# Two layers of sixteen experts: where the sums back to the tokens stand, the last pair as whole fp32 numbers, and the order of the layer norm behind them

## The reference, cut to what matters

```python
def _expert_choice_ffn(u, w_router, w_g, w_u, w_d):
    cap = CAPACITY_FACTOR * n // N_EXPERTS          # 64 tokens for each of 16 experts
    aff = softmax(einsum('bnd,de->ben', u, w_router), axis=1)
    gate, idx = lax.top_k(aff, cap)
    xe = u[bidx, idx]
    hg, hu = einsum(xe, w_g), einsum(xe, w_u)
    ye = einsum(silu(hg) * hu, w_d) * gate[..., None]
    return jnp.zeros_like(u).at[bidx, idx].add(ye)
...
h = _layer_norm(ALPHA * h + m[5] * experts(h), ln_ffn_g, ln_ffn_b)     # end of layers 0 and 1
...
hn = rmsnorm(h, attn_norm[0]); h = h + hybrid_ab(hn, ...)              # first step of the second network
```

## Time and profile before

| what | value |
|---|---|
| time, median of 3 runs | 2934.12 us (2933.55 to 2934.4) |
| span of the profiled execution | 2932.9 us |
| mean granted PE clock | 0.975 |
| PE busy | 2717.6 us, 93% |
| DVE / ACT / POOL busy | 1156.8 / 813.5 / 119.7 us |
| chain that ended last | PE 75%, DMA 12%, DVE 8%, ACT 3% |

### The profile page before, as it was taken

How to read it: one execution, slowest core, us unless ns; L and a number is a source line. 1 busy time by engine, 2 the same in 40 slices (tenths; PEclk the granted TensorE clock), 3 DMA queues, 4 the chain that set the end, 5 groups by cost and what they waited for, 6 DMA issues and landing times.

```text
span 2932.9 us, 32767 instructions
## 1 busy us (share of the span) xinstructions
PE 2717.6 (93%) x13760; PEld 1779.9 (61%) x13760; DVE 1156.8 (39%) x1700; ACT 813.5 (28%) x1249; POOL 119.7 (4%) x120
## 2 busy tenths in 40 slices
PE   6898899998899989998879999999999999999998
PEld 4555444433378544343337777878778766787886
DVE  4465512211264442111135654323244577532333
ACT  3253211100132121100024324212232467532222
POOL 1211100000000200000010010000010000000000
PEclk8999999999999989999999999999999899999999
DMA  8980799999922189999982203231341200132220
GB/s 305 325 282 16 284 415 428 427 422 421 419 99 108 44 342 424 423 419 428 428 329 92 86 29 115 72 124 57 107 130 41 69 1 1 65 115 86 95 85 36
DMA packets 125586, 601.03 MB, mean 205 GB/s; under 512 B 7408, under 2 KB 12848, under 8 KB 100608
## 3 DMA queue, kind: packets, MB, share of 16 engines
q1 hardware_dynamic: 120128, 584.27, 50.3%
q0 software_dynamic: 5312, 14.68, 1.6%
HBM read 596.83 MB, written 2.10 MB: 204 GB/s over the span
## 4 chain that ended last, share of the span: by engine, by line
PE 75%; DMA 12%; DVE 8%; ACT 3%; issue 1%; POOL 0%; DVEq 0%; ACTq 0%; POOLq 0%
PE psum L302 72%; DMA weight_ring<-in_w_exp_down 4%; DMA scratch<-in_w_exp_down 4%; PE psum L317 4%; ACT scratch L290 3%; DVE scratch L252 3%; DMA scratch<-in_w_exp_up 2%; DMA weight_ring<-in_w_exp_up 2%; DMA weight_ring<-in_w_mod 1%; DVE scratch L265 1%; DVE scratch L3773 1%; DVE h L252 1%; DVE scratch L1448 0%; DVE scratch L1947 0%; DVE scratch L1945 0%
## 5 line engine op out<-in xcount | busy, mean ns | idle before, releaser
L302 PE MATMUL psum<-scratch,scratch 128*128 128x512 f32 (+12 forms) x9404 | 1869.6, 397 | 64.7 <-DVE scratch L252 18.4
L302 PEld LDWEIGHTS psum<-scratch,scratch 128*128 128x128 f32 (+5 forms) x9404 | 1365.2, 178 | 539.3 <-issue 203.6
L302 PE MATMUL psum<-weight_ring,scratch 128*64 128x512 f32 (+2 forms) x2752 | 649.7, 612 | 71.8 <-DMA weight_ring<-in_w_exp_down 29.8
L290 ACT ACTIVATE scratch<-psum 128x512 f32<-128x512 f32 (+5 forms) x384 | 221.6, 577 | 1037.7 <-PE psum L317 554.8
L302 PEld LDWEIGHTS psum<-weight_ring,scratch 128*64 128x64 f32 (+2 forms) x2752 | 210.0, 141 | 457.7 <-issue 372.5
L252 DVE TENSOR_TENSOR scratch<-weight_ring,scratch 128x2048 fp32r<-128x2048 f32 (+2 forms) x110 | 241.9, 2199 | 480.2 <-ACT scratch L290 478.6
L290 ACT ACTIVATE scratch<-weight_ring 128x2048 fp32r<-128x2048 f32 (+2 forms) x122 | 218.7, 1793 | 570.3 <-PE psum L302 547.2
L252 DVE TENSOR_TENSOR scratch<-scratch,psum 128x512 f32<-128x512 f32 x92 | 63.3, 688 | 511.8 <-PE psum L302 510.4
L252 DVE TENSOR_TENSOR scratch<-scratch,scratch 128x512 fp32r<-128x512 f32 (+13 forms) x359 | 198.3, 552 | 63.1 <-ACT scratch L290 43.2
L317 PE MATMUL psum<-consts,scratch 128*128 128x128 f32 x1116 | 168.5, 291 | 37.1 <-DVE scratch L252 20.2
L252 DVE TENSOR_TENSOR scratch<-psum,scratch 64x512 f32<-64x512 f32 (+7 forms) x109 | 77.6, 712 | 306.8 <-PE psum L302 302.3
(11 more groups left out here) (107 smaller groups left out, 721.7 us busy)
## 6 DMA issues: line engine op xcount, KB each, us to landing
weight_ring<-in_w_exp_down SPq DMA_DIRECT2D x46, 2048.0 KB, 13.8
weight_ring<-in_w_exp_up SPq DMA_DIRECT2D x43, 2048.0 KB, 15.7
weight_ring<-in_w_exp_gate SPq DMA_DIRECT2D x42, 2048.0 KB, 15.7
weight_ring<-in_ffn_w SPq DMA_DIRECT2D x28, 2048.0 KB, 7.7
weight_ring<-in_w_mod SPq DMA_DIRECT2D x24, 2048.0 KB, 9.6
scratch<-in_w_exp_gate SPq DMA_DIRECT2D x22, 2048.0 KB, 15.8
scratch<-in_w_exp_up SPq DMA_DIRECT2D x21, 2048.0 KB, 15.8
scratch<-in_w_exp_down SPq DMA_DIRECT2D x18, 2048.0 KB, 14.2
```

Of the source, the lines that this page charges most:

```text
L290: A.eng.activation(out, in_, fn, **kw).then_inc(*A.mark(*names))
L302: ins = T.eng.matmul(out, lhsT, rhs, start=start, stop=stop)
```

## The change: what it does

The way back has now two parts beside the experts, and its last pairs are handled apart. A sum (`plus_pe`) also multiplies pair 6 (experts 12 and 13, split as before) into its bank. Two of the sums stand before the down product of expert 14, two before that of expert 15, two behind it, and the last two among the jobs. Pair 7 (experts 14 and 15) is not split: DVE multiplies the down product by row and slot gate in one instruction, and each job ends in one whole fp32 product of `slotsT` and `y`. For that the slot gates of pair 7 must lie on both halves of the partitions, and `gates_pe` makes them by 16 products instead of 4. Sums 4 to 7 name their banks instead of taking the next ones in turn. In the norm of the second layer `gained` of the tile before moves between `stats` and `finish`; `mean` and `diagonals` of tile 0 move ahead of `finish` of tile 3. POOL adds the bias of tiles 0 and 1 only, DVE that of tiles 2 and 3, and POOL makes `units.lo` of the first unit instead of DVE. ACT makes `units.hi` of it behind the norm of tile 0.

```diff
@@ -836,8 +836,6 @@
 class SumNorm(PostNorm):
-    POOLED = NT - 1
-
     def normed(self, t):
@@ -858,15 +856,14 @@
             self.stats(V, t)
+            if after and t == NT - 1:
+                after.mean(V, 0, 1)
+                after.diagonals(V, 0, 1)
+            elif after and t:
+                self.gained(V, t - 1)
             self.finish(V, t)
-            if not after:
-                continue
-            if t == NT - 1:
-                after.mean(V, 0, 1)
-            if t:
-                self.gained(V, t - 1)
         if after:
-            after.diagonals(V, 0, 1)
+            self.gained(V, NT - 2)
             self.gained(V, NT - 1)
@@ -1612,7 +1609,7 @@
-    PARTS = ((0, 4), (4, 6), (6, 8))
+    PARTS = ((0, 4), (4, 6))
     AHEAD = 6
@@ -1691,6 +1688,8 @@
                 yield "turned", (e + 1) // 2
+            if e == E - 1:
+                yield from (("plus", j) for j in jobs[:2])
             if e:
@@ -1703,9 +1702,9 @@
                 yield from (("back", (1, *j)) for j in jobs[4 * (e - 13):4 * (e - 12)])
-        yield from (("plus", j) for j in jobs[:2])
+        yield from (("plus", j) for j in jobs[2:4])
         yield "down", E - 1
-        yield from (("plus", j) for j in jobs[2:self.AHEAD])
+        yield from (("plus", j) for j in jobs[4:self.AHEAD])
         yield from (("back", (2, *j)) for j in jobs)
@@ -1904,19 +1903,18 @@
             {"slots": self.slots_act, "up": self.up_act, "flip": self.flip_act, "rows": self.rows_act, "turned": self.turned_act}.get(what, self.nothing)(A, e)
-        self.down_act(A, E - 1)
         after = self.after
         for t in range(NT):
-            if after and t == NT - 1:
-
+            self.norm.norm_act(A, t)
+            if after and t == 0:
+                after.units.hi(A, 0)
+            if after and t == NT - 2:
                 A.wait_ge(*k.at("end", self.end_key, "pe"))
                 after.square(A, 0)
-            self.norm.norm_act(A, t)
+                after.root(A, 0, 1)
         if after:
-            after.root(A, 0, 1)
             after.square(A, 1)
             after.square(A, 2)
-            after.units.hi(A, 0)
             after.root(A, 1, 3)
@@ -1975,8 +1973,8 @@
                 after.diagonals(V, t0, t1)
-            after.units.lo(V, 0)
             after.chunks_dve(V)
+            V.wait_ge(*k.at("unit split", after.units.n0))
             after.units.lo(V, 1)
@@ -1993,6 +1991,7 @@
                 self.norm.norm_pool(G, t)
+            self.after.units.lo(G, 0)
         G.end(self.end_key)
@@ -2083,6 +2082,15 @@
         pair = 4 * g + pr
+        if pair == E // 2 - 1:
+            for e in range(2):
+                for half in range(2):
+                    for t in range(NT):
+                        end = t == NT - 1
+                        mm(T, bank[64 * half:64 * half + 64, 2 * e:2 * e + 2],
+                           self.onehot[g][:, t, pr * P + 64 * e:pr * P + 64 * e + 64].bitcast(F32), self.aff[:, t, 2 * pair:2 * pair + 2],
+                           t == 0, end, *([("full", key, "gates", *job)] if end and e and half else []))
+            return
         for t in range(NT):
@@ -2093,7 +2101,8 @@
         V.wait_ge(*k.at("full", key, "gates", *job))
-        copy(V, self.slot_gate[:, 2 * pair:2 * pair + 2], k.psum.of((key, "gates", *job))[:, 0:2], ("free", key, "gates", *job))
+        own = slice(0, 4, 3) if pair == E // 2 - 1 else slice(0, 2)
+        copy(V, self.slot_gate[:, 2 * pair:2 * pair + 2], k.psum.of((key, "gates", *job))[:, own], ("free", key, "gates", *job))
     def slots_pe(self, T, t):
@@ -2220,15 +2225,15 @@
             rows_, cols = slice(64 * half, 64 * half + 64), slice(half * HALF, (half + 1) * HALF)
-            tt(V, self.y[q, cols], k.psum.of((key, "down", e))[rows_, :], self.row[rows_, cols], ALU.mult, (key, "y", e, half),
-               *([("free", key, "down", e)] if half else []))
+            names = [(key, "y", e, half)] + ([("free", key, "down", e)] if half else [])
+            out, bank, row = self.y[q, cols], k.psum.of((key, "down", e))[rows_, :], self.row[rows_, cols]
+            if e >= E - 2:
+                stt(V, out, bank, self.slot_gate[rows_, e:e + 1], row, ALU.mult, ALU.mult, *names)
+            else:
+                tt(V, out, bank, row, ALU.mult, *names)
+        if e >= E - 2:
+            return
         hi, lo, y, gate = self.y_parts(e)
-        if e == E - 1:
-            for half in range(2):
-                s = slice(4 * half, 4 * half + 4)
-                V.wait_ge(*k.at(key, "y hi", e, half))
-                stt(V, lo[:, s], y[:, s], gate, hi[:, s].bitcast(F32), ALU.mult, ALU.subtract, (key, "y split", e, half))
-            return
         V.wait_ge(*k.at(key, "y hi", e))
@@ -2237,33 +2242,51 @@
         i, t, half = job
+        if i == len(self.PARTS):
+            name = (self.end_key, "out", t, half)
+            if 2 * t + half >= self.AHEAD:
+                self.plus_pe(T, (t, half))
+            T.wait_ge(*k.at(self.key, "y", E - 1, half))
+            mm(T, k.psum.of(name), self.slotsT[:, E // 2 - 1, t * P:(t + 1) * P].bitcast(F32), self.y[:, half * HALF:(half + 1) * HALF],
+               False, True, ("full", *name))
+            return
         p0, p1 = self.PARTS[i]
-        T.wait_ge(*k.at(self.key, "y split", 2 * p1 - 1, *([half] if p1 == E // 2 else [])))
+        T.wait_ge(*k.at(self.key, "y split", 2 * p1 - 1))
         T.wait_ge(*k.at("free", self.key, "slots", t, 0))
         T.wait_ge(*k.at("free", self.key, "slots", t, 1))
-        last = i == len(self.PARTS) - 1
-        name = (self.end_key, "out", t, half) if last else (self.end_key, "part", *job)
-        if last and 2 * t + half >= self.AHEAD:
-            self.plus_pe(T, (t, half))
-        bank = k.psum.of(name) if last else k.psum.take(T, name)
+        name = (self.end_key, "part", *job)
+        self.pairs_pe(T, k.psum.take(T, name), p0, p1, t, half, True, ("full", *name))
+
+    def pairs_pe(self, T, bank, p0, p1, t, half, first, *names):
+
         for pair in range(p0, p1):
...
             end = pair == p1 - 1
-            mm(T, bank, s, self.high[:, pair, 4 * half:4 * half + 4, :], pair == p0 and not last, False)
-            mm(T, bank, s, self.low_of(pair)[:, half * HALF:(half + 1) * HALF], False, end, *([("full", *name)] if end else []))
+            mm(T, bank, s, self.high[:, pair, 4 * half:4 * half + 4, :], pair == p0 and first, False)
+            mm(T, bank, s, self.low_of(pair)[:, half * HALF:(half + 1) * HALF], False, end and bool(names), *(names if end else ()))
     def plus_pe(self, T, job):
...
         T.wait_ge(*k.at(self.end_key, "back", 1, t, half))
-        bank = k.psum.take(T, (self.end_key, "out", t, half))
+        i = 2 * t + half
+        if i == 0:
+            self.first_bank = k.psum.turn[0, 8]
+        own = {4: 7, 5: 3, 6: 2, 7: 6}.get(i)
+        if own is None:
+            bank = k.psum.take(T, (self.end_key, "out", t, half))
+        else:
+            b = (self.first_bank + own) % 8
+            bank = k.psum.take(T, (self.end_key, "out", t, half), (b, b + 1))
         mm(T, bank, k.ident, k.h[:, t, half * HALF:(half + 1) * HALF], True, False)
+        T.wait_ge(*k.at(self.key, "y split", E - 3))
+        self.pairs_pe(T, bank, E // 2 - 2, E // 2 - 1, t, half, False)
```

10 lines of the change are left out of this document (3 added, 7 removed).

## The result

| | before | after |
|---|---|---|
| time, median of 8 runs each | 2933.84 us | 2943.73 us (2937.58 to 2945.09) |
| ratio | | 1.0027, 95% interval 1.0019 to 1.0036 |
| span of the profiled execution | 2932.9 us | 2943.3 us |
| PE / DVE / ACT / POOL busy | 2717.6 / 1156.8 / 813.5 / 119.7 us | 2727.2 / 1153.3 / 809.0 / 121.9 us |

The change makes the kernel slower by 0.27%. Laid on the 2934.12 us of the front, the ratio gives 2942.0 us (2939.7 to 2944.7). The forecast was 2939.0. So 2942.0 lies above the forecast's own 2937.5 to 2940.5 and on the very edge of the stated range of 2934.0 to 2942.0. By the forecast's own bound of 2940.0 slower came, to which it gave 0.26; the lower end of the interval, 2939.7, lies just under that bound.

The account below looks back on a forecast made before the run. PE was busy 93% of the span, so time was won or lost only where PE stands still. 0.6 + 4.4 = 5.0 us on 2932.9 gave 2937.9, 2939.1 with the 1.2 around it, stated as 2939.0; range 2934.0 to 2942.0.

Parts of the forecast that it names:

- The norm: Second layer's norm: DVE's shifts of tiles 1 and 2 and tile 0's diagonal wait for POOL; 4.4 us later.
- The first rival: Second layer's norm: small shifts go free, only the diagonal is held; +2.8 us, 2937.5 in all; chance 0.15.
- the second: Second layer's norm: DVE and POOL do not hold each other up; -0.1 us, 2934.1 to 2934.6; chance 0.17.
- Ahead of the last down product: End of the expert layers: costlier sums make the last down product end 0.86 us later in the first, 1.20 in the second.
- Behind it: Last down product to first statistics: two sums and a job instead of four sums and a job, 0.92 us less.
- The gates: Slot gates of pair 7 at expert 8: 3.0 us more PE work per layer, covered by waits for weights; taken as 0.
- The turning over: Behind the first layer: PE waits for a bank of tile 3 with twelve transposes behind it; 0.6 us later.
- PE cold: Second layer's products on the diagonals: longer pause leaves PE's clock low; up to 4.4 us more, likelier 2941.2; chance 0.18.
- The 1.2 us around the span: Whole kernel: difference between the span (2932.9) and the median of the runs (2934.12), taken to stay.
- The sum: Whole kernel: 0.6 us for the first layer's turning over plus 4.4 for the second layer's norm, 5.0 in all.

Follow-up runs that it names:

- e9: The changed kernel with shifts as an instruction with one SBUF tensor input and the first unit's low part on DVE, not POOL; norm 21.64 us, second stretch 58.96 us.
- e6: The changed kernel with only DMA issues on POOL in the second layer's closing stretch, DVE doing its work; norm 23.64 us, second stretch 59.64 us.
- e4: The kernel before with only the norm's part of the change; ratio to the kernel before 1.0023 (1.0014 to 1.0033).
- b2: The kernel before with DVE adding the bias of tile 2 and ACT making the unit's high part behind the norm of tile 1; ratio 1.0000.
- e5: The changed kernel with its last four sum banks in another order and the ring's turn moved on by one; first stretch 47.28 us, second 66.18 us.
- e1: The changed kernel with each shift made by an instruction with one SBUF tensor input instead of two; norm 24.47 us, second stretch 62.43 us.
- e1_finish_first: The changed kernel with each tile's reciprocal and shift ahead of `gained` of the tile before; norm 26.04 us, second stretch 61.80 us.

## Why the prediction was right and where it was off

- *The norm*: the mechanism named is the one that the runs show. The shifts are held until POOL ends, the diagonal ends with POOL's 128x2048 (4.50 us, as worked out), and e9, which takes away only the two overlaps, gives back 4.25 of 4.68. The size needs care, since the forecast's 4.4 has the 0.28 of the later statistics in it. From the first statistics on it stands for 4.1, and measured is 25.89 - 21.2 = 4.7, 0.6 more. Up to the statistics of tile 3 it was 3.70 for the forecast's 3.6. The stalls were smaller than priced (1.59 and 1.97 for 2.1 to 2.2 each), but DVE still waited 0.56 for ACT's root ahead of the first. The rest of the 0.6 came behind, most of it between the diagonal's end and PE's run (6.84 for 6.5).
- *The first rival* (small shifts go free) is refuted by the rows at 1529.11 and 1534.52, *the second* (DVE and POOL do not hold each other) by these and the one at 1540.20, and by e6.
- *Ahead of the last down product*, 0.86 and 1.20 us: mis-sized. By up piece to sums it was 0.5 (24.61 to 25.12) and 0.6 (24.88 to 25.49). The new sums stand 1.43 apart as priced (1498.32 to 1499.75), so more of them than I allowed lay in waits for weights. With the next term the statistics thus start 0.35 sooner in the first layer (forecast 0.06 sooner) and 0.25 sooner in the second (forecast 0.28 later).
- *Behind it*, -0.92: measured 4.67 to 3.81 in both layers, -0.86. Right.
- *The gates*, 0: no loss seen. From the first conv product to expert 15's up piece of the second layer, a piece that holds the gates, the three kernels with few gate products (before, e4, b2) took 661.6 to 664.0 us, the eleven others 660.0 to 663.5. Right, to within the 3 to 4 us by which these differ among themselves.
- *The turning over*, 0.6: the mechanism was right and its size too (from the first sum to the first conv product, e5 with the banks mended has 21.92 us, the kernels with the change's banks and the upper clock 22.49 on average: 0.6). But the piece from the norm's end to the first conv product grew by 2.26 (before 820.30 to 825.82, after 822.15 to 829.93): 1.2 to 1.3 is the clock, since the transposes stand in one block that PE reached at 0.66, and some 0.4 stays open; part of it is there in e5 too, whose first product waits 4.08 us for DVE where it was 3.72.
- *PE cold*, my third rival at 0.18: this is the step that failed. I set it beside the forecast as something that happens or does not, and argued that the 16 records of tile 0 would warm PE up. In this execution they did not: the clock was 0.50 in all windows to 1550, at a price of 1.1 us, and in the first layer, where I had no such term at all, of 1.2. In executions of other kernels whose PE work there is the same, or the same but for the banks, it cost nothing (e5 in the second layer, e1, e6 and e1_finish_first in the first). It belongs in the sum, as a term with a range.
- *The 1.2 us around the span*: each run of the change lies 1.7 to 1.8 us above its own span, and the runs of the kernel before that were timed beside e1 lie 1.9 to 2.1 above theirs. The 1.2 came from setting three runs against the span of another execution. Since the forecast adds its 5.0 to the median of these three, only tenths hang on it.
- *The sum*: of the 7.4 us, 2.3 are clock, and the 5.1 that are left stand against the forecast's 5.0. That agreement is partly luck: some 0.8 less ahead of the statistics in the two layers was made up by 0.6 more in the norm and 0.4 more in the turning over.

## What to carry to other kernels

Ask of every instruction moved across the start of a GpSimd one whether VectorE will wait for it. Here the price was what was left of GpSimd's instruction, even for 128x1 with two SBUF inputs, and taking away one such meeting could only move the wait to the next. Judge such a repair by the piece that it works on, not by a longer stretch in which other waits move. Put the clock behind a pause of PE into the sum as a term with a range: here 0 to 2.2 us for the 48 records behind pauses of 8 to 13 us, and which of them came could not be told from the length of the pause. A ring of banks or buffers is state for all stages behind: after a change of how many turns one stage takes, look at the first wait of the next.
